# Order and chunk sizes of the adaLN input stage in a one-core hybrid trunk layer: x loaded first, modulation made in six chunks

## The reference, cut to what matters

```python
def rmsnorm(x, g):
    r = x * lax.rsqrt(jnp.mean(x * x, axis=-1, keepdims=True) + EPS)
    return r * g

mod = jax.nn.silu(cvec) @ w_mod + b_mod          # cvec: c (latent) or c_ctx (context); w_mod 2048 x 12288
sh1, sc1, g1, sh2, sc2, g2 = jnp.split(mod, 6, axis=-1)
h = rmsnorm(x, g_pre1) * (1 + sc1) + sh1         # x: 640 x 2048
proj = h @ w_in                                  # w_in: 2048 x 9216
```

## Time and profile before

| | us |
|---|---|
| median of 3 runs (2848.52 to 2850.75) | 2850.73 |
| the profiled execution, whole | 2848.87 |
| its span, first to last instruction | 2847.3 |
| TensorE matmul busy | 2786.2 (98% of the span) |
| TensorE weight loads busy | 2385.9 (84%) |
| VectorE busy | 2107.0 (74%) |
| ScalarE busy | 1501.5 (53%) |
| DMA | 757.23 MB, mean 266 GB/s |
| mean granted TensorE clock | 0.992 of full |

### The profile page before, as it was taken

The page is one execution under the profiler, slowest core; times in us unless marked ns, Lnnn a source line. Parts: engine busy times, 40 slices in busy tenths (PEclk is TensorE's granted clock), DMA queues, the critical chain, the costliest instruction groups (busy, mean ns, idle before and its releaser), DMA issues.

```text
span 2847.3 us, 40831 instructions
## 1 busy us (share of the span) xinstructions
PE 2786.2 (98%) x14958; PEld 2385.9 (84%) x14958; DVE 2107.0 (74%) x1918; ACT 1501.5 (53%) x1466; POOL 284.2 (10%) x337
## 2 busy tenths in 40 slices
PE   7999999999999999999999996999999999999998
PEld 5688888899999999999988775888888888888886
DVE  2339688796777777763343577888888888888888
ACT  4411221125556556552232455777777777777776
POOL 1000000002111111100000001100111101100100
PEclk9999999999999999999999997999999999999999
DMA  9877677664343444364443767999999999999997
GB/s 368 314 266 255 220 258 264 225 227 137 121 123 119 123 123 123 102 207 126 122 143 119 293 213 275 365 395 395 395 395 396 395 391 394 392 388 387 393 395 296
DMA packets 258405, 757.23 MB, mean 266 GB/s; under 512 B 20248, under 2 KB 127296, under 8 KB 194000
## 3 DMA queue, kind: packets, MB, share of 16 engines
q1 hardware_dynamic: 234272, 650.01, 61.4%
q0 software_dynamic: 23120, 100.71, 10.9%
q10 hardware_dynamic: 928, 5.33, 0.5%
HBM read 700.61 MB, written 55.37 MB: 266 GB/s over the span
## 4 chain that ended last, share of the span: by engine, by line
PE 91%; DVE 3%; DMA 2%; ACT 1%; issue 1%; SPq 0%; DVEq 0%; ACTq 0%; POOL 0%; POOLq 0%
PE ps L542 21%; PE ps L544 21%; PE ps L543 21%; PE ps L2402 5%; PE ps L2403 5%; PE ps L2404 5%; PE ps L2569 3%; PE ps L2570 3%; PE ps L2571 3%; PE ps L2259 2%; PE ps L2507 1%; DMA raw<-in_w_mod 1%; DVE rsd L1827 1%; PE ps L2271 1%; PE ps L2282 1%
## 5 line engine op out<-in xcount | busy, mean ns | idle before, releaser
L467 DVE TENSOR_TENSOR we_lo<-raw,we_hi 128x2048 fp32r<-128x2048 f32 x384 | 877.3, 2289 | 113.1 <-ACT we_hi L462 113.0
L462 ACT ACTIVATE we_hi<-raw 128x2048 fp32r<-128x2048 f32 x384 | 736.5, 1918 | 260.9 <-PE ps L544 260.9
L411 ACT ACTIVATE w_hi<-raw 128x2048 fp32r<-128x2048 f32 x115 | 220.0, 1913 | 444.5 <-PE ps L544 356.7
L421 DVE TENSOR_TENSOR w_lo<-raw,w_hi 128x2048 fp32r<-128x2048 f32 x115 | 263.5, 2291 | 191.4 <-ACT w_hi L411 186.8
L542 PE MATMUL ps<-we_hi,xs_lo 128*128 128x512 f32 x1024 | 399.7, 390 | 0.1
L544 PE MATMUL ps<-we_hi,xs_hi 128*128 128x512 f32 x1024 | 399.2, 390 | 0.0
L543 PE MATMUL ps<-we_lo,xs_hi 128*128 128x512 f32 x1024 | 399.2, 390 | 0.0
L2402 PE MATMUL ps<-hi,w_lo 128*128 128x320 f32 x1152 | 365.6, 317 | 0.9 <-ACT stage L1122 0.9
L2403 PE MATMUL ps<-lo,w_hi 128*128 128x320 f32 x1152 | 356.1, 309 | 0.0
L2404 PE MATMUL ps<-hi,w_hi 128*128 128x320 f32 x1152 | 356.0, 309 | 0.0
L1614 DVE SCALAR_TENSOR_TENSOR mod_acc<-mod_raw,sc,mod_acc 128x2048 f32<-128x2048 f32 x120 | 276.7, 2348 | 3.3
(11 more groups left out here) (445 smaller groups left out, 4765.6 us busy)
## 6 DMA issues: line engine op xcount, KB each, us to landing
raw<-in_w_e_gate SPq DMA_DIRECT2D x128, 1024.0 KB, 7.5
raw<-in_w_e_up SPq DMA_DIRECT2D x128, 1024.0 KB, 7.9
raw<-in_w_e_down SPq DMA_DIRECT2D x128, 1024.0 KB, 11.6
raw<-in_w_in SPq DMA_DIRECT2D x144, 512.0 KB, 5.6
mod_raw<-in_w_mod SPq DMA_DIRECT2D x64, 1024.0 KB, 5.4
raw<-in_w_mod SPq DMA_DIRECT2D x64, 512.0 KB, 7.4
raw<-in_w_o SPq DMA_DIRECT2D x64, 512.0 KB, 4.9
d_proj<-g_stage POOLq DMA_DIRECT2D x32, 320.0 KB, 2.4
```

The lines of the kernel that those rows point to most:

```text
L411: act.activation(w_hi[:, j % NHL, s], raw[:, slot, s], ACT.Copy).then_inc(hi_ready, 1 if fine else 2)
L421: dve.tensor_tensor(w_lo[:, j % NHL, s], raw[:, slot, s], w_hi[:, j % NHL, s].bitcast(F32), ALU.subtract).then_inc(lo_ready, 1 if fine else 2)
L462: act.activation(we_hi[:, k % NEH, :], raw_slot(k), ACT.Copy).then_inc(hi_ready, 2)
L467: TTn(we_lo[:, k % NEH, :], raw_slot(k), we_hi[:, k % NEH, :].bitcast(F32), ALU.subtract).then_inc(lo_ready, 2)
```

## The change

- x is loaded by SyncE, ahead of every other load of that queue, each tile with a semaphore of its own.
- The rows of x are multiplied by the reciprocal root mean square on VectorE (`normalise`, in place, 128 x 2048), and TensorE turns them by plain transposes with the identity. ScalarE loads the table for the square root ahead of the first tile.
- Shift and scale are made in six chunks of 2, 2, 4, 4, 2, 2 k tiles. A unit stays 1 MB. In a chunk of two k tiles a unit holds 256 columns of 8 k tiles of rows (rows of 1 KB in memory, 8 matmuls of 256 columns), two units to a sum; in a chunk of four it is as before.
- `START` becomes: units 0 to 3, v0, 4 to 11, v1, 12 to 19, v2, 20 to 27, v3, 28 to 31. A piece of values waits for its half of v, not for the whole.
- The order on TensorE is written anew, with no `turn_rows` inside a piece.

```diff
+CHUNKS = ((0, 2), (2, 2), (4, 4), (8, 4), (12, 2), (14, 2))
+PARTS = [w for _, w in CHUNKS for _ in range(2)]
+FIRST = [sum(PARTS[:i]) for i in range(2 * NCH + 1)]
...
+            for t in range(TT):
+                src = a["x_sample"][0][t * P:(t + 1) * P, :] if t < TT - 1 else a["x_prompt"][0]
+                sp.dma_start(x_in[:, t, :], src).then_inc(x_sems[t], 16)
             for i, (what, n) in enumerate(START):
                 if what == "mod":
-                    start_load(i, wide(w_mod, i % NRAW, n % 4, n // 4 % 2 * D + n // 8 * 512))
+                    start_load(i, mod_parts(i % NRAW, n))
...
-            load_x(0)
-            load_x(1)
             for t in range(TT):
                 square(t)
-                if t + 2 < TT:
-                    load_x(t + 2)
                 if t:
                     take_x(t - 1)
-            row_out(0)
-            v_split_hi(act, 0, 0)
-            row_out(1)
-            v_split_hi(act, 0, 1)
             take_x(TT - 1)
...
+            for c, (k0, w) in enumerate(CHUNKS):
+                if c and w == 4:
+                    v_split_hi(act, k0 // 4, 0)
+                    v_split_hi(act, k0 // 4, 1)
+                row_out(2 * c)
+                row_out(2 * c + 1)
+                if c and w == 2 and k0 % 4 == 0:
+                    v_split_hi(act, k0 // 4, 0)
+                    v_split_hi(act, k0 // 4, 1)
+                act.wait_ge(S["a1_ready"], c + 1)
+                for k in range(k0, k0 + w):
                     tokens(k)
+                    if k < 2:
+                        v_split_hi(act, 0, k)
...
-                TS(A["diag"][:, t % 2, :], ident[:], stats[:, 16 + t:17 + t], None, ALU.mult).then_inc(S["xn_ready"], 1)
+                TS(x_in[:, t, :], x_in[:, t, :], stats[:, 16 + t:17 + t], None, ALU.mult).then_inc(S["xn_ready"], 1)
...
-                        last = pe.matmul(ps[:, 4 + kq, (k % 4) * P:(k % 4 + 1) * P], x_in[:, t, k * P:(k + 1) * P],
-                                         A["diag"][:, t % 2, :], start=True, stop=True)
+                        last = turn(ps[:, 4 + kq, (k % 4) * P:(k % 4 + 1) * P], x_in[:, t, k * P:(k + 1) * P])
...
-                for kk in range(4):
-                    last = pe.matmul(ps[32 * kk:32 * kk + 32, bank, :], c2[:, 4 * kp + kk, :],
-                                     raw[:, i % NRAW, kk * 512:kk * 512 + 512], start=(kp == 0), stop=(kp == 3))
+                for kk in range(ks):
+                    j = kk % 4
+                    last = pe.matmul(ps[32 * j:32 * j + 32, bank, 0:n], c2[:, ks * part + kk, :],
+                                     raw[:, i % NRAW, kk * n:kk * n + n], start=(part == 0 and kk < 4),
+                                     stop=(part == w - 1 and kk >= ks - 4))
...
             pe.wait_ge(S["c_ready"], 1)
+            for t in range(TT - 1):
+                turn_x(t)
+            turn_parameters()
             mod_unit(0)
             mod_unit(1)
-            turn_parameters()
-            for m in range(2, 8):
-                mod_unit(m)
-                if m == 7:
-                    turn_rows(0)
-                if m >= 3:
-                    turn_x(m - 3)
+            turn_x(TT - 1)
+            turn_rows(0)
+            mod_unit(2)
+            mod_unit(3)
             turn_rows(1)
...
-            mod_units(8, 11)
+            mod_units(4, 5)
             first_values(0)
-            mod_units(11, 12)
+            mod_units(5, 7)
+            turn_rows(2)
             first_values(1)
-            mod_units(12, 13)
+            mod_units(7, 8)
+            turn_rows(3)
+            mod_units(8, 9)
             first_values(2)
-            turn_rows(2)
-            mod_units(13, 16)
-            first_values(3, amid=3)
+            mod_units(9, 10)
+            first_values(3)
+            mod_units(10, 12)
+            turn_rows(4)
+            mod_units(12, 16)
+            turn_rows(5)
+            first_values(4)
             mod_units(16, 18)
-            first_values(4)
-            mod_units(18, 20)
             first_values(5)
-            mod_units(20, 21)
+            mod_units(18, 19)
             first_values(6)
-            turn_rows(4)
-            mod_units(21, 24)
-            first_values(7, amid=5)
-            mod_units(24, 26)
+            mod_units(19, 20)
+            turn_rows(6)
+            first_values(7)
+            mod_units(20, 24)
+            turn_rows(7)
             first_values(8)
-            mod_units(26, 28)
+            mod_units(24, 25)
             first_values(9)
-            mod_units(28, 30)
+            mod_units(25, 26)
+            turn_rows(8)
+            mod_units(26, 27)
             first_values(10)
-            turn_rows(6)
-            mod_units(30, 32)
-            first_values(11, amid=7)
-            for k in range(12, KT):
-                first_values(k)
+            mod_units(27, 28)
+            turn_rows(9)
+            first_values(11)
+            first_values(12)
+            mod_units(28, 31)
+            turn_rows(10)
+            mod_units(31, 32)
+            turn_rows(11)
+            first_values(13)
+            first_values(14)
+            first_values(15)
```

More of the change, by code:

```diff
@@ L66 @@
 MOD_FROM = [sum(MOD_TILES[:n]) for n in range(8)]
-START = [("mod", m) for m in range(8)] + [("v", 0)] + [x for h in range(1, 4) for x in [
-    ("mod", 8 * h + m) for m in range(4)] + [("v", h)] + [("mod", 8 * h + m) for m in range(4, 8)]]
+CHUNKS = ((0, 2), (2, 2), (4, 4), (8, 4), (12, 2), (14, 2))
+NCH = len(CHUNKS)
+PARTS = [w for _, w in CHUNKS for _ in range(2)]
+FIRST = [sum(PARTS[:i]) for i in range(2 * NCH + 1)]
+SUM_OF = {m: i for i in range(2 * NCH) for m in range(FIRST[i], FIRST[i + 1])}
+START = []
+for _c, (_k0, _w) in enumerate(CHUNKS):
+    START += [("mod", m) for m in range(FIRST[2 * _c], FIRST[2 * _c + 1])]
+    if _c and _w == 4:
+        START.append(("v", _k0 // 4))
+    START += [("mod", m) for m in range(FIRST[2 * _c + 1], FIRST[2 * _c + 2])]
+    if _k0 % 4 == 0 and (_w == 2 or _c == 0):
+        START.append(("v", _k0 // 4))
 MOD_AT = {m: i for i, (what, m) in enumerate(START) if what == "mod"}
@@ L1517, in tokens @@
                 TTn(lo[:, k, :], xT[:, k, :], hi[:, k, :].bitcast(F32), ALU.subtract).then_inc(S["tok_lo"], 1)
-            dve.wait_ge(S["rows_turned"], 2)
-            own.done(dve.tensor_copy(A["cols_b"][:], ps[:, 4, 0:48]))
-            own.done(dve.tensor_copy(A["cols2"][:], ps[:, 5, 0:105]))
-            own.settle()
             for t in range(TT):
-                norm_diagonal(t)
+                normalise(t)
                 if t:
                     take_x(t - 1)
-            v_split_lo(dve, 0, 0)
-            mod_columns(0)
-            v_split_lo(dve, 0, 1)
             take_x(TT - 1)
-            mod_columns(1)
+            dve.wait_ge(S["rows_turned"], 2)
+            own.done(dve.tensor_copy(A["cols_b"][:], ps[:, 3, 0:48]))
+            own.done(dve.tensor_copy(A["cols2"][:], ps[:, 3, 64:169]))
+            own.settle()
             dve.sem_inc(phase, 1)
@@ L1541, in take_values @@
                     dve.tensor_copy(v_stage[:, t, :], ps[:, t, :]).then_inc(S["bank_taken"], 1)
-            for h in range(4):
-                if h:
-                    v_split_lo(dve, h, 0)
-                    v_split_lo(dve, h, 1)
-                    mod_columns(2 * h)
-                    mod_columns(2 * h + 1)
-                if h == 3:
+            for c, (k0, w) in enumerate(CHUNKS):
+                if c and w == 4:
+                    v_split_lo(dve, k0 // 4, 0)
+                    v_split_lo(dve, k0 // 4, 1)
+                mod_columns(2 * c)
+                mod_columns(2 * c + 1)
+                if c and w == 2 and k0 % 4 == 0:
+                    v_split_lo(dve, k0 // 4, 0)
+                    v_split_lo(dve, k0 // 4, 1)
+                if c == NCH - 1:
                     dve.sem_inc(S["mod_used"], CREDIT["mod_used"])
                     dve.sem_inc(S["m_row_ready"], 2)
-                for k in range(4 * h, 4 * h + 4):
+                for k in range(k0, k0 + w):
                     tokens(k)
+                    if k < 2:
+                        v_split_lo(dve, 0, k)
             split_lo(dve, Q_V, 4)
@@ L2215, in _ @@
             expert(NE - 1, 1, True)
[L2216 removed]
+            dve.wait_ge(S["g2_loaded"], 48)
             def gain(i, t):
@@ L2293, in turn_rows @@
                     pe.wait_ge(S["a1_ready"], s // 2)
-                for n in range(4):
+                for n in range(PARTS[s]):
                     last = pe.matmul(ps[:, bank, at0 + 2 * n:at0 + 2 * n + 2], A["m_rows"][:, s % 2, n * P:(n + 1) * P],
@@ L2353, in first_values @@
                         last.then_inc(S["bank_done"], 1)
-                    if amid is not None and t == 1:
-                        turn_rows(amid)
                 if k % 4 == 3:
```

75 lines of the change are left out of this document (38 added, 37 removed).

## The result

The changed kernel takes 2880.95 us (median of 4 runs, 2879.58 to 2881.87), the kernel before in the same session 2849.62 us (4 runs, 2847.55 to 2850.75): ratio 1.0111, 95% interval 1.0099 to 1.0124, 31.3 us slower. That is clear of the noise of the runs, though small, 1.1%. The forecast was 2866, the range 2853 to 2878: the sign is right, the size lies 3 us outside the range. The profiled execution has a span of 2878.0 us, 30.7 more than before.

The account below looks back on a forecast made before the run. It took transfers and TensorE, coupled by four slots, to bound the stage ahead of the second pass; 9.5 (walk) + 2 (clock, x step) + 4 (clock, later waits) = 15.5 on 2850.7 gave 2866 us, range 2853 to 2878.

Parts of the forecast that it names:

- What bounds the kernel: Stage ahead of the second pass: bound by transfers and TensorE, coupled by four slots; its end moves the kernel's one for one.
- Step 1, the x step: Start to x's transposes: tile 0 normalised at 14.2, `turn_x(3)` ends at 26.0, queue empty from 27 to 29.2.
- Step 2, v0's slot: Up to the first values, at 39.1: SyncE waits for v0's slot, queue empty from 40.2 to 43.5.
- Step 3, the walk from piece 0: First values to stage end: 39.1 + 89.6 work + 5.0 + 10.0 + 5.0 of waits = 148.7.
- the 1% added to the walk: Counting the kernel before came out 1% short; with that added the stage ends at 149.8, 9.5 later.
- The clock: Low clock costs 2 in the x step, and two falls of 2.2, rounded to 4, over four later waits.
- Rival 3, the clock falls at every long wait: All four waits bring a fall: 9.5 + 6 + 11.2 = 26.7 slower, 2877; chance 0.10.
- Narrow units and rows of 1 KB: Units of 256 columns cost TensorE as wide ones; their transfers are 10% slower, 0.27 each, not waited for: 0.
- rival 4: Narrow units cost by count of matmuls, not columns: 15.5 + 13 = 28.5 slower, 2879; chance 0.05.

Follow-up runs that it names:

- e14: The kernel before with 14 extra 128x128 products in TensorE's wait ahead of unit 2: 2849.64 us, ratio 0.9999.
- e1: The changed kernel with extra 128x128 products, results unused, ahead of nine long waits of TensorE: 2868.67 us, ratio 1.0067 to the kernel before.
- e12: The changed kernel with both halves of v0 split ahead of the first chunk's tokens: 2882.13 us, ratio 1.0110 to the kernel before.
- e13: The kernel of e6 with v0's halves split where the kernel before has them, ahead of the last tile of x: 2887.18 us, ratio 1.0131.
- e2: The changed kernel with VectorE's and ScalarE's small parameter work moved from behind the last tokens to behind the fourth chunk's: 2877.52 us, ratio 1.0100.
- e3: The changed kernel with pieces 1, 3 and 7 moved behind the turn of their chunk's scale: 2876.87 us, ratio 1.0095 to the kernel before.
- e4: The changed kernel with the 64 KB identity loaded ahead of x on SyncE's queue: 2875.79 us, ratio 1.0091 to the kernel before.
- e9: The changed kernel with e2, e3, e4, some extra products, and the splits of v1 and v2 behind the shift's read-out and columns: 2868.19 us, ratio 1.0066.
- e5: The x part of the change alone, with chunks of four k tiles and TensorE's order from unit 8 on as before: 2859.66 us, ratio 1.0040.
- e6: The change's chunks and TensorE order alone, with x loaded and multiplied by the diagonal as in the kernel before: 2889.26 us, ratio 1.0142.
- e10: The kernel before with chunks of 4, 4, 4, 2, 2 and VectorE's parameter work behind the third chunk's tokens: 2847.54 us, ratio 0.9994.

## Why the prediction was right or wrong

The forecast was 15.5 us slower, and the kernel is 31 slower. Step by step, by its own terms:

- **What bounds the kernel (right).** Both bounds are near; e14 points to the transfers up to piece 0.
- **Step 1, the x step (right but for the identity).** `normalise` took 1.29, a tile 1.97 to 2.13 at the full clock, the queue was empty near 28 to 30, as forecast. Tile 0 was ready at 16.4, not at 14.2: the late identity was missed. The low clock of tile 0 cost 1.5 (tile 2 at 23.60, in e1 at 22.06), for which the forecast had 2. Unit 0 was used about 2.6 late, unit 4 was issued at 32.5 instead of 28.6 and landed at 40.3, not at 35.2; so piece 0 came at 42.2, where the walk without its clock term had 39.1.
- **Step 2, v0's slot (place right, weight nothing).** SyncE stood there, but the queue was nearly empty for only 1.3 us near 45.5, where 3.3 was forecast, and e12 and e13 put the cost of the slot at 0 to 2 us.
- **Step 3, the walk from piece 0 (right in nearly every term).** Forecast: 5.0 for read-outs, 10.0 for pieces behind a turn, 5.0 for units 13 to 15. Measured: 4.9, 9.8, 5.1 (4.2 for units 13 to 15 and 0.9 for unit 23), with the 3.4 ahead of pieces 4 and 8 met to 0.01. Missed is the `v_stage` wait of 3.5: the walk ended at `first_values(15)` and took for granted that what lay hidden behind four and a half pieces of the kernel before would stay hidden behind three (e2: 3.6). "Nothing behind it waits for a fixed time" was false for this wait. Work was 90.9 (e1), 1.3 above the 89.6, which the 1% added to the walk made good.
- **The clock (the step that failed).** "I take two falls of 2.2, rounded to 4", for the waits from piece 0 on. Measured in its place: 11.6 from piece 0 to the pass (half of 23.1 us of work; 102.5 less e1's 90.9) and 2.5 behind the pass, 14.1 in all. The 2 for the x step was about right (1.5). Two things were wrong. The clock was low behind every one of the long waits (2.9, 2.4, 3.4, 3.4 and the missed 3.5; PEclk 0.50 at 41, 58, 90, 122 and 169), not behind two; that two of the four would bring a fall was my estimate, and no run shows it. And a fixed price of 2.2 to 2.8 per fall was the wrong form: once low it stayed low while further waits kept coming, though five of the six waits from 71 to 90 us are of 0.72 to 1.85 us. It lasted 20 us, 74 to 94, of which TensorE worked 12.1 and so lost 6.1. The argument that waits of 1.2 had left the clock alone before did not carry over to this order.
- **Rival 3, the clock falls at every long wait (nearest to what came).** It had 26.7 us, 2877, and a chance of 0.10. Its 11.2 for the four waits is close to the 11.6; its 6 for the x step was too much and the `v_stage` wait was missing.
- **Narrow units and rows of 1 KB (right).** A narrow unit took 0.97 to 1.07 at the full clock, as a wide one; rival 4 is out. Its rows moved at 348 GB/s where 2 KB rows make 387, 10% less, as forecast. That a narrow unit is never waited for was not so: unit 4 was, for 2.9 us.

Closing the sum: 15.5 + 1.1 (piece 0 late by 3.1, of which the forecast had 2 as clock) + 10.1 (the clock behind it, 11.6 + 2.5 in place of 4) + 3.5 (`v_stage`) + 0.2 (work, 1.3 in place of 1.1) = 30.4, and 30.7 is measured. The clock is the largest term of the miss; with it alone the sum would have been 25.6, inside the range, and with `v_stage` 29.1, just outside.

**Why the change loses at all.** Before, behind piece 0 the units stand between pieces one to three at a time, a slot is used about when it lands, and half a piece covers each turn of a scale: 4.9 us idle. After, chunks of two k tiles come where TensorE has no piece to put in front of the wait, and the two large chunks run four units in a row. What is gained at the start (piece 0 10.1 earlier, of which 7.8 is only work moved behind it: 90.9 against 83.1) is paid for with 18.4 of idle time and 11.6 of clock: -10.1 + 7.8 + 18.4 + 11.6 = 27.7. Why the gains of e1, e2, e3 and e4 don't add up was followed in e3 and e9 only, where waits for units and read-outs grew as others went. Which order of units and pieces would be free of it wasn't found, and stays open.

## What to carry to other kernels

Price the clock by stretch, not by wait: here, where short waits followed one another, all the work between them ran at half speed (20 us in the changed kernel, 17 in e5), and cheap extra products in the waits were a quick test of it. Before a stage is made shorter at its start, ask what paces the rest: with the order of before, 9.5 us saved on the transposes made the kernel 11 us slower (e5), with the order of the change they made it 9 faster (e6 against the whole change). And work that is hidden behind the end of a stage has to be asked for again when that end is made shorter (`v_stage`). Small chunks at the end of the stage, where there is work in stock to cover their hand-overs, brought the pass forward by 3.0 us (e10), though nothing that the time shows; small chunks at its start alone were not tried.

## What the runs showed of the hardware that I had not expected

- Extra products made the kernel 12.2 us faster (e1), where the clock was low in and behind waits (mean PEclk from piece 0 to the pass 0.85, with the products 0.97); in the kernel before they changed nothing (e14, 0.6 us slower by the medians, within the noise).
- The clock stayed at 0.50 for 20 us (74 to 94), though no wait in them was longer than 3.4 us and the other four were of 0.72 to 1.85.
- A small load on one queue, issued at the same time, landed 2.3 us later when the other queue moved x in rows of 8 KB than when it moved units in rows of 2 KB (10.2 against 7.9); issued first on the stream's own queue it no longer was the last to land (e4, TensorE's first product at 5.7).
- The granted clock is shown as 1.00 from 0 to 17 us in each trace, but the pace of the instructions says otherwise: the kernel before took 3.64 us for its first two units, where one at 28.09 took 1.06, and the changed kernel ran 12 instructions of its transposes in the 2 us from 17 us, 16 later. Early in a trace the length of a known instruction is the safer reading.
